# Hybrid GLA and forgetting-attention block on one core: the first projections run before shift1 is known, and its share is added later

## What is computed

```
mod = silu(c) @ w_ada + b_ada            # w_ada: 2048 x 12288
shift1, scale1, gate1, shift2, scale2, gate2 = split(mod, 6)
h    = rms_norm(x, g_norm1) * (1 + scale1) + shift1
proj = h @ w_in                          # w_in: 2048 x 16416
gq, gk, gv, gg, ga_low, fq, fk, fv, f_logit, gate_a, gate_b = split(proj)
o_a  = rms_norm(gla(gq/16, gk, gv, log_a), g_gla_out) * silu(gg)   # 4 heads
o_b  = forgetting_attention(fq, fk, fv, log_f)                     # 16 heads
x   += gate1 * ((sig(gate_a)*(o_a @ w_proj_gla) + sig(gate_b)*(o_b @ w_proj_fox)) @ w_out)
x   += gate2 * (relu(h2 @ w_ff1)**2 @ w_ff2)       # h2 like h, of x, with shift2, scale2
return rms_norm(x, g_final)
```

## Time and profile before

| what | us |
|---|---|
| median of 3 runs | 1890.29 |
| lowest, highest | 1889.85, 1892.19 |
| the profiled execution, its own time | 1895.73 |
| its span in the profile | 1894.0 |
| PE busy in it | 1853.2 (98%) |
| DVE, ACT busy | 1186.5 (63%), 836.8 (44%) |
| HBM read | 425.34 MB, 226 GB/s over the span |

### The profile page before, as it was taken

How to read it: one execution, slowest core, us unless ns; L and a number is a source line. 1 busy time by engine, 2 the same in 40 slices (tenths; PEclk the granted TensorE clock), 3 DMA queues, 4 the chain that set the end, 5 groups by cost and what they waited for, 6 DMA issues and landing times.

```text
span 1894.0 us, 21600 instructions
## 1 busy us (share of the span) xinstructions
PE 1853.2 (98%) x8387; PEld 1489.3 (79%) x8387; DVE 1186.5 (63%) x1327; ACT 836.8 (44%) x1042; POOL 19.3 (1%) x40
## 2 busy tenths in 40 slices
PE   6989999999999999999999998999999999999998
PEld 2458788888888888888888886888888888888886
DVE  5865566665667666666666777775555555555555
ACT  2335454554545445344444444443344344434443
POOL 1000000000000000000000000000000000000000
PEclk9989999999999999999999998999999999999999
DMA  9978589699897897898899784886665666666663
GB/s 387 381 233 245 168 193 241 202 217 230 203 208 242 230 240 225 236 248 273 280 254 259 247 305 156 267 272 207 196 184 186 189 199 188 182 196 190 187 189 124
DMA packets 208239, 428.92 MB, mean 226 GB/s; under 512 B 18053, under 2 KB 34533, under 8 KB 207754
## 3 DMA queue, kind: packets, MB, share of 16 engines
q1 hardware_dynamic: 206744, 423.99, 76.1%
q10 hardware_dynamic: 1138, 3.50, 0.5%
q0 software_dynamic: 256, 0.05, 0.0%
HBM read 425.34 MB, written 2.10 MB: 226 GB/s over the span
## 4 chain that ended last, share of the span: by engine, by line
PE 93%; DMA 3%; DVE 2%; issue 1%; ACT 0%; SPq 0%; POOL 0%; DVEq 0%; POOLq 0%
PE ps L1599 85%; DMA first<-in_w_ada 3%; PE ps L1583 1%; PE ps L1703 1%; PE ps L1557 0%; DVE acch L1050 0%; PE ps L1755 0%; DVE wlo L1097 0%; PE ps L1524 0%; PE ps L1522 0%; PE ps L1567 0%; PE ps L1700 0%; DVE xT L1443 0%; PE ps L1712 0%; PE ps L1652 0%
## 5 line engine op out<-in xcount | busy, mean ns | idle before, releaser
L1097 DVE TENSOR_TENSOR wlo<-raw,whi 128x1024 fp32r<-128x1024 f32 x604 | 738.7, 1225 | 630.7 <-ACT whi L638 629.4
L638 ACT ACTIVATE whi<-raw 128x1024 fp32r<-128x1024 f32 x604 | 639.3, 1060 | 955.8 <-PE ps L1599 811.0
L1599 PE MATMUL ps<-whi,hT 128*128 128x512 f32 x2304 | 734.6, 395 | 1.3 <-ACT hT L625 1.3
L1599 PEld LDWEIGHTS ps<-whi,hT 128*128 128x128 f32 x2304 | 435.1, 189 | 100.6 <-issue 10.3
L1599 PE MATMUL ps<-wlo,hT 128*128 128x512 f32 x1152 | 450.4, 391 | 0.0
L1599 PE MATMUL ps<-whi,obT 128*128 128x512 f32 x1280 | 404.2, 394 | 2.2 <-ACT obT L947 1.2
L1599 PE MATMUL ps<-whi,oaT 128*128 128x512 f32 x1248 | 389.3, 390 | 0.0
L1599 PEld LDWEIGHTS ps<-whi,obT 128*128 128x128 f32 x1280 | 241.7, 189 | 54.2 <-issue 2.4
L1599 PEld LDWEIGHTS ps<-whi,oaT 128*128 128x128 f32 x1248 | 234.3, 188 | 49.0 <-issue 0.5
L1599 PEld LDWEIGHTS ps<-wlo,hT 128*128 128x128 f32 x1152 | 217.8, 189 | 44.6 <-issue 0.7
L1599 PE MATMUL ps<-wlo,obT 128*128 128x512 f32 x640 | 250.2, 391 | 0.0
(11 more groups left out here) (219 smaller groups left out, 749.6 us busy)
## 6 DMA issues: line engine op xcount, KB each, us to landing
raw<-in_w_ff SPq DMA_DIRECT2D x256, 512.0 KB, 4.2
raw<-in_w_in SPq DMA_DIRECT2D x224, 512.0 KB, 6.2
raw<-in_w_ada SPq DMA_DIRECT2D x128, 512.0 KB, 4.8
first<-in_w_ada SPq DMA_DIRECT2D x64, 512.0 KB, 13.9
raw<-in_w_in SPq DMA_DIRECT2D x64, 256.0 KB, 6.4
raw<-in_w_proj_fox SPq DMA_DIRECT2D x32, 512.0 KB, 5.7
raw<-in_w_proj_gla SPq DMA_DIRECT2D x32, 512.0 KB, 5.8
raw<-in_w_out SPq DMA_DIRECT2D x32, 512.0 KB, 5.3
```

The lines of the kernel that those rows point to most:

```text
L638: nc.scalar.activation(parts(g)[0][:], raw[POS_G[g] % RING][:], ACT.Copy).then_inc(s_hi, 1)
L1097: V.tensor_tensor(rest[:], raw[POS_G[g] % RING][:], top[:].bitcast(F32), ALU.subtract).then_inc(s_lo, 1)
L1599: i = T.matmul(ps[bank(name, t)][:], src[:, kt, hl, tk], w[:, k, :], start=(kt == 0 and n == 0), stop=(kt == KT - 1 and n == 2))
```

## The change

1. **Order of the first groups.** Groups 0 and 1 are now scale1 (kt 0-7, kt 8-15), groups 2 and 3 shift1. `norm1` takes only the scale: h without shift1 stands for kt 0-7 after 16 pieces and for kt 8-15 after 32. Which pieces PE shares (12 of 16 in each group) is the same code result as before.
2. **HEAD runs earlier.** `LOAD_AT` puts the loads of all 24 HEAD units and of units 24 and 25 between pieces 13 and 60; their matmuls run in pairs between pieces 17 and 58.
3. **h is then made again with shift1** for FOX and everything later: ACT scales xT in place (`norm1_scale`, 16 operations) and writes the high part with the shift as bias (`shift_hi`, 16), DVE the low part (`shift_lo`, 16; the 16 of `xs`, L1083, are gone).
4. **HEAD's missing row** shift1 @ W is computed in FOX. 24 more loads of 512 KB ride through `raw` (16 with gv's and gg's weights of one kt each, 8 with qk's), DVE multiplies them by shift1's column and adds them up (`accv` 16 x 128x1024, `accq` 16 x 128x512), PE sums over partitions with `ones` (`shift_sum`, iterations 98, 100 and 122) and DVE adds the row to gv, gg, gq and gk (`shift_add`). Silu of gg moves behind that.
5. **Riders.** From iteration 48 to 119 there is a rider on every second iteration, two of three for the shift; afterwards on two of five until the sixth group of modulation is through. Groups 6 and 7 stay.
6. The transposes of x stand at pieces 6 to 13, the norm's sums at pieces 2 and 4; `small` is loaded four units later; qk's copy, turn and evacuation in FOX loop 0 are five iterations later (copy at 5, turn at 7, evacuation at 8, where before 0, 2 and 3).

```diff
-PIECE += [(_n, _k, _rows) for _k in range(0, KT, _rows)]
+PIECE = [(_n, _k) for _n in range(FIRST) for _k in range(KT)]
-EARLY = (12,)
+LOAD_AT = [13, 14, 15] + [17 + 7 * _i // 4 for _i in range(9)] + [32] + [33 + 2 * _i for _i in range(1, 12)] + [58, 60]
+    if _g < UG * len(HEAD):
+        for _r in range(max(LOAD_AT[_g | 1] + 3, KT + 1), PIECES):
+            RUN[_r] = _g + 1
+SHIFTS = KT + UG
+G_SHIFT = G_FOX + 24
...
+        if G_SHIFT <= g and j < SHIFTS and (n % 3 < 2 or g < free):
+            RIDE_AT[g] = ("w", j)
...
+        g += 3 if g < G_SHIFT else 2 if j < SHIFTS or n % 2 else 3
...
-                col = STARTS[n // 2] * P + (0 if n % 2 else D)
+                col = n % 2 * 2 * NB + (D if n < 2 else 0)
...
-                nc.scalar.activation(hT[:, kt, 0, :], xT[:, kt, :], ACT.Identity, scale=gcol[:, 0, kt:kt + 1],
-                                     bias=modc[:, 0, kt:kt + 1]).then_inc(s_hh, 1)
+                nc.scalar.activation(hT[:, kt, 0, :], xT[:, kt, :], ACT.Copy, scale=gcol[:, 0, kt:kt + 1]
+                                     ).then_inc(s_hh, 1)
...
+            def shift_lo(kt):
+                dve.wait_ge(s_hh, KT + kt + 1)
+                V.scalar_tensor_tensor(hT[:, kt, 1, :], xT[:, kt, :], modc[:, 0, kt:kt + 1],
+                                       hT[:, kt, 0, :].bitcast(F32), ALU.add, ALU.subtract).then_inc(s_hl, 1)
...
+            def shift_piece(j, pos):
+                if j < KT:
+                    rows = [(accv[:], r[:], j, 2)]
+                else:
+                    rows = [(accq[:], r[:, k, :], KU * (j - KT) + k, 1) for k in range(KU)]
...
+            def shift_sum(g):
+                pe.wait_ge(s_wacc, 2 * (KT if n < 2 else SHIFTS))
+                if n < 2:
+                    i = T.matmul(ps[7][:], ones[:], accv[:, n, :], start=True, stop=True)
+                else:
+                    for j in range(4):
+                        i = T.matmul(ps[7][:, j:j + 1], accq[:, j * P:j * P + P], ones[:, 0:1], start=True, stop=True)
...
-                if 11 <= p < 27 and p % 2:
-                    norm_turn((p - 11) // 2)
+                if 6 <= p < 14:
+                    norm_turn(p - 6)
```

More of the change, by code:

```diff
@@ L86, in full @@
 def full(p):
-    n, k, rows = PIECE[p]
-    return p > P_LAST[n] - 2 or rows == 1 and k in (0, 7)
+    n, k = PIECE[p]
+    return p > P_LAST[n] - 2 or k in (0, 7)
 def pieces_pe(p):
@@ L141, in pieces_done, with sums_at, ride, ride_all @@
     return 2 * (PIECES + m * KT + k + 1)
-def ride(m, g0, step, sums=None):
-    for k in range(KT):
[L146 to L155, removed]
+def sums_at(m, g):
+    for h in range(1 if m < GATE1 else 2):
+        MOD_AT[g + 2 * h] = (m, h)
+    return g + (0 if m < GATE1 else 2)
+def ride(m, g0, step, sums):
+    for k in range(KT):
+        RIDE_AT[g0 + step * k] = ("a", (m, k))
+    return sums_at(m, sums)
+def ride_all():
+    g, m, k, j, n, free = G_FOX + 1, 0, 0, 0, 0, 0
+    while m < 6:
+        if G_SHIFT <= g and j < SHIFTS and (n % 3 < 2 or g < free):
+            RIDE_AT[g] = ("w", j)
+            j += 1
+            if j == KT:
+                SHIFT_AT[g + 3], SHIFT_AT[g + 5] = 0, 1
+            if j == SHIFTS:
+                SHIFT_AT[g + 3] = 2
+        elif g >= free:
+            RIDE_AT[g] = ("a", (m, k))
+            k += 1
+            if k == KT:
+                at = g + 3
+                while any(a in SHIFT_AT for a in (at, at + 2)):
+                    at += 1
+                free = sums_at(m, at)
+                m, k = m + 1, 0
+        n += 1
+        g += 3 if g < G_SHIFT else 2 if j < SHIFTS or n % 2 else 3
+    assert j == SHIFTS and not set(SHIFT_AT) & set(MOD_AT)
+    return free
+_g = max(ride_all(), G_OUT - 5)
 _g = ride(6, _g, 2, G_FF + 6)
-_g = ride(7, _g, 2)
+_g = ride(7, _g, 2, _g + 2 * KT)
+def sums_before(g):
+    return ADA0 + sum(a < g for a in MOD_AT), sum(a < g for a in SHIFT_AT)
 NORM2_UNITS = (4, 9, 14)
@@ L538, in _ @@
                     loaded += 1
-            for pos in range(ROW_G, len(STREAM)):
-                if pos == G_FOX:
+            for pos in range(loaded, len(STREAM)):
+                if pos == G_FOX + 4:
                     sp.wait_ge(s_zero, 1)
@@ L701, in fox_stage, with shift_silu @@
                     take_turned(("fk", it), ((fk, 1.0),))
+            def shift_silu(g):
+                if SHIFT_AT.get(g - 1) == 1:
+                    act.wait_ge(s_wadd, 2)
+                    nc.scalar.activation(gg[0][:], gg[0][:], ACT.Silu).then_inc(s_silu, 1)
             def gla_stage(it, u):
@@ L1328, in gla_heads @@
                     gla_head(it - 1, u - 3)
-            for g in range(split - LEAD, G_FOX):
-                lo(g + LEAD)
             for it in range(4):
@@ L1337, in _ @@
                     mod(g)
+                    shift_add(g)
                     if it:
@@ L1564, in sum_first @@
                     pe.wait_ge(s_mod, 2 * n - 2)
-                for j in range(CHUNKS[n // 2]):
+                for j in range(8):
                     c = n % 2 * 8 + j
@@ L1630, in _ @@
                     run += 1
-            for g in range(run, G_FOX):
-                row_unit(g)
             def small_cols():
```

287 lines of the change are left out of this document (175 added, 112 removed).

## The result

The changed kernel takes 1896.72 us (median of 8 runs, 1895.03 to 1900.02), the kernel before 1891.62 us (8 runs, 1889.85 to 1893.25): ratio 1.0023, 95% interval 1.0014 to 1.0032. It is slower by 5 us, or 0.23%, where 1888.3 us, and so a faster kernel, was forecast. The profiled execution took 1897.15 us, with a span of 1895.4.

The account below looks back on a forecast made before the run. TensorE was taken to bound the kernel. From the profiled 1895.73 us, -7.5 (start), +3.0 (new sums) and +2.5 (FOX loads) gave 1893.7, or 1888.3 as a median; 8 in 10 range 1880.5 to 1898.

Parts of the forecast that it names:

- What bounds the kernel: Whole kernel: TensorE is 93% of the chain that ended last; time changes with its idle gaps, half clock and work.
- Part 1: Start: units from 39.0 us instead of 62.77, so FOX starts at about 152.5 to 153.0 instead of 160.5: -7.5 us.
- the plan of the row: PE's work in the start: first unit at 39.0 us, then 104.6 us of work, last shared piece ending at 143.6.
- named as a refutation: Last sum of the start, at 146 us: taking 1.8 us would show the clock forecast wrong; 3.4 was expected.
- -12.5: Start: the gain in us should the clock not fall at the last sum, which then takes 1.8 us.
- -5.4: Whole kernel: the profiled execution lies 5.4 us above the median of the runs, taken off to give a median.
- Part 2: PE's path: two sums of 512 columns by ones, 2.04 us, and four columns, 0.92 us: +3.0 us.
- Part 3: FOX: new shift loads fall behind by 2 and 6 us in loops 1 and 3; stalls 0 to 5, +2.5 us.
- Nil with landings under 8 us: FOX: no PE waits together with unit landings under 8 us would show the forecast for its loads wrong.
- only put off: DVE in FOX: the 24 shift riders replace modulation riders that are merely postponed; no time was charged for those.
- B: Rival, chance 0.28: no stall in FOX, clock back early, start gains 8 to 12.5 us; 1883 us (1881 to 1885.5).
- C: Rival, chance 0.22: odd FOX loops bound by loads, or late loads carry into GLA; stalls 8 to 16 us, centre 1896.

Follow-up runs that it names:

- k13_before_thin_sum152: Kernel before, with modulation group 1 riding every third iteration from 104 to 149, its sum at 152, two of five only from 152: 1898.45 us, ratio 1.0033.
- k10_before_dense_sum152: Kernel before, with modulation group 1 riding from iteration 109, two of five from 122, and its sum at 152: 1904.55 us, ratio 1.0072.
- k7_before_dense: Kernel before, with modulation pieces riding two of five iterations from 122, sums at 162, 202, 242 and 285: 1896.49 us, ratio 1.0012.
- the start alone: Changed kernel without shift loads, shift sums and additions, its modulation pieces riding where they do in the kernel before: 1883.09 us, ratio 0.9943.
- k2_no_shift: Changed kernel without shift loads, shift sums and additions, modulation pieces riding exactly as in the changed kernel: 1894.88 us, ratio 1.0016.
- k4_qk2_cols: Changed kernel with the loads of qk of head 2 taken from head 0's columns, riders as they are: 1891.55 us, ratio 0.9994.
- k1: Changed kernel with riders after FOX moved: every third iteration while GLA's heads are fetched, every second in MIX: 1891.17 us, ratio 0.9992.
- k6a_placed: Changed kernel, riders every second iteration, every fourth where columns are slow, sums five iterations after their last rider: 1889.84 us, ratio 0.9991; again 1887.46 us, ratio 0.998.

## Why the prediction was wrong, point by point

- **What bounds the kernel**: right. Time moved only with PE's work, PE's gaps and PE's clock. Not all slow clock stands behind a gap, as I had read it: the spell in FOX's loop 0 has none ahead of it. The list of waits of before gave no hint of GLA, since there the lateness ended in ACT's waits and not in PE's.
- **Part 1, the start, -7.5**: the plan of the row was right to 0.8 us (first unit at 39.0, shared pieces to 142.8 for 143.6), the clock was not. The sum as written, 149.6 plus 1.7 to 3.4, gives 151.3 to 153.0 and not 152.5 to 153.0, so -7.5 was its far end. I counted a half-clock sum of 3.4 us and up to 3.4 on units; the sum took 1.95, which I had named as a refutation, and the half clock came behind it, a loss of 1.7 in the 10 us with a mean of 0.83. So -12.0 against -7.5 is 1.6 at the sum, 1.7 at the units and 1.2 in the row and the gap. It lies next to the -12.5 that I had named for a clock that stays up, but the clock did fall; that the two agree is chance. The 1.6 more in FOX's loop 0, the shorter spell there, I had not seen at all.
- **What that gain is worth against a median**: wrong. I took 1895.73 as what the sum is made against, and brought it to the median with -5.4. But the changed kernel's profiled execution lay 0.4 us above its median, so the offset didn't carry over. The cause shows in the three runs that keep the start of before. Behind the same wait the last sum of k13_before_thin_sum152 reads, against 3.41 us in the earlier trace rows,

```profile
120.57 1.95 PE L1579 MATMUL ps<-ones,acch 128*128 128x1 f32 x16 [2.63 <-DVE acch L1062]
...
243.03 0.44 PE L1712 MATMUL ps<-ncrow,ones_r 2*128 2x384 f32 x1
```

  The sum is at full clock, the slow spell behind it ends at 126.6 us instead of 130.8, the one in FOX's loop 0 at 208.6 instead of 212.7, and FOX loop 1's scores come 3.6 us earlier than in the profile of before (4.0 in k10_before_dense_sum152, but only 0.8 in k7_before_dense, whose slow spells are as long as those of before). So the profile of before holds more half clock than every execution has; in one series 16 of its 27 runs lay between 1889.7 and 1891.6 us and 9 between 1893.1 and 1894.8. A gain that consists in part of slow clock removed is then worth less than the profile shows: some 10 us of median, as the start alone measured (10.4 against 1893.47, its series' median of before), not 13.6.
- **Part 2, the new sums, +3.0**: right to 0.5 us; 1.71 us for the wide ones and 0.82 for the four columns by the leads, and 2 us between the run without shift work and the changed kernel.
- **Part 3, FOX's loops, +2.5**: wrong in size, inside its range. No PE wait in FOX, with median landings of 6.6 to 6.9 us in 390 to 460 us, where, against the earlier trace rows, the same share moves more:

```profile
390.00:460.00 70.00, 70.00 (x331) 57.27 (x330) 48.97 (x70) 37.51 (x60) 0.00 (x0) 1.00 0.96 235
```

  I had charged the new loads nearly the price of the loop that they ride in; they read head 0's columns, and between 450 and 480 us, where the qk ones are, the share even fell (0.93 at 277 GB/s, before 0.98 at 255). Nil with landings under 8 us was what I had named as a refutation: the term had charged for loads that the queue took without PE waiting.
- **The step that failed**: the change's description says that the riders put off in FOX are made up behind it, in two of five iterations, and I gave this no term. I followed riders to GLA's edge and treated them as "only put off". So the step took a term at nothing without a reason. Work put off on a full queue has to be priced where it lands: there loads already had a share near 0.95, the first sum behind FOX had moved from 121 to 152, and DVE's queue holds 2.5 us of products right ahead of its last piece. That is 10.4 us, and 2.1 more in MIX and OUT, where PE waits 1.44 us (before: nothing) and 2.10 (before 1.03) for `wlo`.
- **The sum of it**, in terms of the profiles: -13.6 + 2.5 + 10.4 + 2.1 = +1.4, and 1897.15 - 1895.73 = 1.4. In terms of medians, with the start at -10 to -10.4: +4.6 to +5; measured 5.1. The median of before itself lay between 1891.32 and 1893.47 in the series, so the agreement to 0.5 is closer than these numbers carry. Against the forecast of 1888.3 the 8.4 us of error are -6.1 (start), -0.5 (sums), -2.5 (FOX), +12.5 (GLA, MIX and OUT, no term) and +5.0 (the step from the profile to the median).
- **Rivals**: B's mechanism in the start and in FOX was what happened; C's time (1896) came true for another reason, in another place, and it is by C's width alone that 1896.72 lies inside 1880.5 to 1898: luck. C had the loss in GLA in one sentence, loads that carry over into its first qk units, but without shift loads the stall stays (k2_no_shift), so it isn't carried over from them.
- By the Trainium skill, page "DMA: Bandwidth & Descriptors", section "Bandwidth", the 16 engines' ports have a ceiling of 435 GB/s. As an estimate from that figure, the 36 loads of a FOX loop need 43 us of its 77, and the loads have room. The changed kernel's FOX, without a PE wait, fits this better than my term did, but the share of 0.96 at 235 GB/s doesn't, nor does its GLA: a share of 0.98 at 203 GB/s between 530 and 560 us, and faster landings from nothing but other columns (k4_qk2_cols).

## What to carry to other kernels

When a change postpones background work, write down the new slot of every piece and of every consumer that moves with it, and price each in the stage where it lands, not in the one that it leaves. A consumer on the critical engine (here a sum over what another engine has just accumulated) needs a distance that covers that engine's worst lateness, and the queue ahead of its last input has to be read in order; three iterations were enough for the sum at 162 with the dense riders (k7_before_dense), and cost 4.3 us at 152 with the thin ones (k13) and 10.4 to 10.7 with the dense ones. So neither a number of iterations nor a density is safe by itself; the place counts too. Before a gain is read off one profile, ask whether what is removed happens in every execution.

## What the runs showed of the hardware

- Waits of the same length are followed by different clocks. After 2.26 us in the start of the kernel before, the sum took 1.95 us and the half clock began behind it (mean 0.61 in 54 to 62 us); in k7_before_dense, whose start is the same, it began with the sum (3.37 us; mean 0.57 in 54 to 62 us). After 2.63 us the sum took 3.41 us or 1.95, and the spell ended 10.4 or 6.1 us after the sum's start. In OUT waits for `wlo` of 2.02 to 2.52 us had no slow clock behind them in seven runs (after, k1, k2, k6a_placed, k7, k10, k13: a mean of 1.00 over the next 13 us and more), while behind one of 1.79 us in k4_qk2_cols the clock was at half from 1182 to 1186 us. Behind the start, the four longest waits at a sum (2.67, 3.87, 4.61, 4.63) each had a sum of 3.57 or 3.58 us behind them, at half clock; the one of 2.43 had a sum at full clock with the spell behind it, that of 1.98 one that was slow in part (1.56 for 1.02). So no length of wait can be named here that decides it. By the Trainium skill, page "TensorE: Matmul & The Clock Gate", section "Part 1: The HAM clock gate", how many matmuls run slow at a kernel's start differs from run to run of the same kernel; these rows agree, and show it inside the kernel too.
- The clock also falls without a wait: in FOX's loop 0, behind eight matmuls of 17 rows, in every profile of the case (0.57 over 8 us before, 0.79 after).
- Loads of equal bytes and equal rows cost differently by the columns they read: 7.0 us against 9.1 to landing for head 2's qk units, by reading head 0's columns instead.
- Riders don't cost by their number but by where they ride: 96 modulation pieces and 24 shift pieces fit without a PE wait between 150 and 1147 us (k6a_placed), and the same ones in the changed kernel's more even row cost 12 us there. (Behind 1150 us k6a_placed has waits of 2.52 and 1.42 us; the changed kernel has 2.10.)
